# Hybrid encoder, layer 0: the end of the recurrent stage reordered, with part of the output product among the scan steps

## The chip, the cores and the metric
One core of a Trainium2 chip, one launch. The metric is the device time in microseconds (us). PE is TensorE, PEld its weight loads, DVE VectorE, ACT ScalarE, POOL GpSimd, SP the queue that issues the loads.

## What is computed
Two encoder layers on x (512 tokens, 1024 wide) with 256 memory tokens. The change touches layer 0's mixer:
```python
for t in tokens:                       # both directions, 8 heads of 64
    sa = S @ -kk[t]
    S = S*w[t] + outer(sa, kk[t]*a[t]) + outer(v[t], k[t])
    y[t] = S @ r[t]
y = rms_norm(y_fwd + y_bwd, out_gain)  # over each head's 64
a_out = (y + sum(r*k*r_k)*v) * g       # g = sigmoid(gl) @ g2
b_out = u * spatial_gate(v_sgu)
x = x + concat(a_out, b_out) @ ab_w_out
```

## The kernel before, in words
All large products run as three float32r products of high and low parts. A weight slab (4 blocks of 128 rows, 512 columns, 1 MB) is loaded by SP into WRAW[i % 2], ACT copies its high part (`split_hi`, L330), DVE subtracts the low part (`split_lo`, L338), and PE multiplies (`gemm_pe`, L373). `fence` is the number of the first slab of the output product "ab". It has four slabs: rows 512 to 1023 (the SGU half, whose input HHI/HLO[4:8] is ready before the recurrent stage) for both column halves, then rows 0 to 511 for both. Each slab is 48 matmuls in four banks.

The recurrence runs in chunks of 64 tokens, for four pairs of heads, j = 0 to 3 (`pair_pe`, `pair_act`, `pair_dve`, `pair_pool`). A pair is:
- gram (L884, L896; `gram_dve`): products of AR, BET and KAP; DVE masks them out of PSUM into AI, UU, GBR, GKA, GKR, adds the identity to AI and UU (L1233, L1235) and writes TT (L1237);
- five levels `lv` of an inversion by doubling: PE UU x AI (L990), DVE XX (L1282), PE with XX and TT (L1004, L1007), ACT copies UU, TT (L1122, L1126);
- the tail: WU, RT, PT, QT, YL (L1023, L1031, L1061).

After each half level stand one side step s = 0 to 9 (`side_pe`, `side_act`: the bonus sum, LoRA products and turns for this and the next pair) and one scan step of the pair before (`chain_pe`, `chain_dve`; L913 the state, L921 the output). DVE prepares the next pair's operands in levels 2 to 4 (L1153 to L1192), POOL makes BET (`beta_pool`) and multiplies PT and RT by decay ends (`decay`). Every order is written out by hand, each engine's queue runs in order, and semaphores tie them.

After the fourth pair: seven scan steps alone (`chain_end_pe`), a meeting of the four engines, then `fin_*`: squares, a bones product per pair (L1305), Sqrt on ACT, RECIPROCAL on DVE (L1335), gain, bonus, gates (L1306, g), high and low parts. SP waits for the last pair's QT products before it loads slab `fence`; the slabs and X share the space of the stage's tiles.

## Time and profile before

| what | value |
|---|---|
| median of 3 runs | 1855.76 us (1854.86 to 1858.3) |
| the profiled execution | 1856.78 us, span 1855.0 us |
| PE, DVE, ACT, POOL busy | 95%, 53%, 41%, 6% of the span |
| mean granted clock | 0.988 |
| four pairs | 169.3 to 386.4 us |
| last scan steps | 386.4 to 394.2 us |
| up to the end of "ab" | 394.2 to 459.6 us |

A row gives the line of the kernel, the engine, the operation and output<-input. In groups, the columns are busy us, mean ns of one, and idle time of the engine just before them with what ended it. "issue" is time in which the engine waited for nothing that the profile shows. PEclk is the granted TensorE clock as a share of 2.4 GHz.

### The profile page before, as it was taken

Reading aid. Unit: us, or ns where it says so; the run is one execution under the profiler, and the core shown is the slowest. Engines: PE = TensorE matmul, PEld = TensorE weight load, DVE = VectorE, ACT = ScalarE, POOL = GpSimd, SP = SyncE. Lnnn points to the kernel's source line nnn. Section 1 sums busy time; section 2 is a strip of 40 time slices with the busy share of each in tenths; the row PEclk is TensorE's granted clock in tenths of the full one; section 3 lists DMA queues with packets and bytes.
Section 4 is the critical chain, followed back from the end, with each engine's and each line's share of the span. In section 5 each row is a group of like instructions: output and inputs, shape, how many; then the busy total and the mean of one; then the engine's idle time right before and its main releaser. Section 6 shows DMA issues by size and latency. Waiting matters only on the chain.

```text
span 1855.0 us, 32043 instructions
## 1 busy us (share of the span) xinstructions
PE 1754.3 (95%) x14153; PEld 1439.4 (78%) x14153; DVE 992.3 (53%) x1373; ACT 769.3 (41%) x1182; POOL 108.5 (6%) x87
## 2 busy tenths in 40 slices
PE   6997888889999999999999999989999999999999
PEld 5876777767887788888887887557888878888887
DVE  5477656457534556534645244994634356634552
ACT  4243444334554343413433234873655244422431
POOL 1001221000010000000000022000010000000000
PEclk9999999989999999999999999999999999999999
DMA  7210000033331223333222322002322223222221
GB/s 240 80 46 2 4 4 4 4 137 124 136 114 46 69 91 91 108 98 109 95 69 91 108 76 89 1 1 91 117 98 81 91 68 104 101 91 91 91 89 71
DMA packets 96454, 149.41 MB, mean 81 GB/s; under 512 B 3480, under 2 KB 50171, under 8 KB 96315
## 3 DMA queue, kind: packets, MB, share of 16 engines
q1 hardware_dynamic: 94727, 142.29, 23.3%
q0 software_dynamic: 1296, 4.95, 0.8%
q8 instruction: 111, 1.82, 0.4%
q14 instruction: 29, 0.23, 0.0%
q10 hardware_dynamic: 291, 0.12, 0.0%
HBM read 145.25 MB, written 2.10 MB: 79 GB/s over the span
## 4 chain that ended last, share of the span: by engine, by line
PE 82%; DVE 10%; ACT 4%; issue 3%; DMA 1%; POOL 1%; DVEq 0%; POOLq 0%; SPq 0%; ACTq 0%
PE PS L373 68%; DVE SS L1608 1%; PE PS L531 1%; PE PS L1004 1%; PE PS L1397 1%; PE PS L1366 1%; PE PS L990 1%; DVE WLO L338 1%; PE PS L1031 1%; PE PS L1023 1%; PE PS L636 1%; ACT WHI L330 1%; DMA WRAW<-cross_wq 1%; DVE YQ L1335 1%; PE PS L913 1%
## 5 line engine op out<-in xcount | busy, mean ns | idle before, releaser
L338 DVE TENSOR_TENSOR WLO<-WRAW,WHI 128x2048 fp32r<-128x2048 f32 (+1 forms) x132 | 296.9, 2251 | 455.0 <-ACT WHI L330 455.0
L330 ACT ACTIVATE WHI<-WRAW 128x2048 fp32r<-128x2048 f32 (+1 forms) x132 | 248.1, 1880 | 431.2 <-PE PS L373 404.5
L373 PE MATMUL PS<-HIS,WHI 128*128 128x512 f32 x856 | 333.8, 390 | 1.5 <-DVE SM L1770 1.5
L373 PE MATMUL PS<-HIS,WLO 128*128 128x512 f32 x856 | 333.0, 389 | 0.0
L373 PE MATMUL PS<-LOS,WHI 128*128 128x512 f32 x856 | 333.0, 389 | 0.0
L373 PE MATMUL PS<-WHI,HIS 128*128 128x512 f32 x608 | 238.8, 393 | 4.2 <-DVE WLO L338 3.5
L373 PE MATMUL PS<-WLO,HIS 128*128 128x512 f32 x608 | 237.4, 390 | 0.0
L373 PE MATMUL PS<-WHI,LOS 128*128 128x512 f32 x608 | 237.3, 390 | 0.0
L373 PEld LDWEIGHTS PS<-HIS,WHI 128*128 128x128 f32 x856 | 160.7, 188 | 35.1 <-DVE SM L1770 1.7
L373 PEld LDWEIGHTS PS<-HIS,WLO 128*128 128x128 f32 x856 | 160.7, 188 | 33.7
L373 PEld LDWEIGHTS PS<-LOS,WHI 128*128 128x128 f32 x856 | 160.7, 188 | 33.2 <-issue 0.2
L373 PEld LDWEIGHTS PS<-WHI,HIS 128*128 128x128 f32 x608 | 114.6, 188 | 29.6 <-DVE WLO L338 3.9
L373 PE MATMUL PS<-WHI,GHI 128*128 128x512 f32 x352 | 136.9, 389 | 0.0
L373 PE MATMUL PS<-WHI,GLO 128*128 128x512 f32 x352 | 136.9, 389 | 0.0
L373 PE MATMUL PS<-WLO,GHI 128*128 128x512 f32 x352 | 136.9, 389 | 0.0
L373 PEld LDWEIGHTS PS<-WLO,HIS 128*128 128x128 f32 x608 | 114.6, 188 | 24.0
L373 PEld LDWEIGHTS PS<-WHI,LOS 128*128 128x128 f32 x608 | 114.5, 188 | 23.4
L538 DVE TENSOR_TENSOR X<-X,PS 128x512 f32<-128x512 f32 x64 | 43.1, 685 | 66.3 <-PE PS L373 66.2
L373 PEld LDWEIGHTS PS<-WLO,GHI 128*128 128x128 f32 x352 | 66.1, 188 | 13.8
L373 PEld LDWEIGHTS PS<-WHI,GHI 128*128 128x128 f32 x352 | 66.1, 188 | 13.7
L373 PEld LDWEIGHTS PS<-WHI,GLO 128*128 128x128 f32 x352 | 66.1, 188 | 13.6
L1483 ACT ACTIVATE GHI<-SG 128x512 fp32r<-128x512 f32 x44 | 27.8, 633 | 108.6 <-DVE SG L1503 108.6
(283 smaller groups left out, 2474.1 us busy)
## 6 DMA issues: line engine op xcount, KB each, us to landing
WRAW<-ffn_w_up SPq DMA_DIRECT2D x88, 512.0 KB, 4.7
WRAW<-ffn_w_down SPq DMA_DIRECT2D x20, 1024.0 KB, 5.0
WRAW<-cross_wkv SPq DMA_DIRECT2D x16, 1024.0 KB, 5.1
WRAW<-diff_w_in SPq DMA_DIRECT2D x12, 1024.0 KB, 5.1
WRAW<-ab_w_in SPq DMA_DIRECT2D x10, 1024.0 KB, 5.5
WRAW<-cross_wq SPq DMA_DIRECT2D x8, 1024.0 KB, 5.1
WRAW<-cross_wo SPq DMA_DIRECT2D x8, 1024.0 KB, 5.1
X<-x SPq DMA_DIRECT2D x8, 512.0 KB, 7.2
```

Source lines behind the costliest of these rows:

```text
L330: A.e.activation(part(WHI[i % 3], i), part(WRAW[i % 2], i), ACT.Copy).then_inc(S("w_hi"), 1)
L338: V.e.tensor_tensor(part(WLO[i % 3], i), part(WRAW[i % 2], i), part(WHI[i % 3], i).bitcast(F32), ALU.subtract).then_inc(S("w_lo"), 1)
L373: mm = e.matmul(o, l, r, start=(si == 0 and kk == 0 and q == 0), stop=(si == len(steps) - 1 and kk == nk - 1 and q == 2))
L531: mm = e.transpose(PS[:, norm_bank(b0, k), t * P:t * P + P], xn[:, t, k * P:k * P + P], ident)
L538: V.e.tensor_tensor(o, o, PS[:, bank_base(name, gi) + b, :], ALU.add).then_inc(sem(name, "ev"), 1)
L636: mm = e.transpose(PS[:, bank0 + k % 4, t * P:t * P + P], tok[:, t, k * P:k * P + P], ident)
L913: mm = e.matmul(PS[half(hh), 4, d * HD:d * HD + HD], PT[half(hh), d, o[d][0], :], QT[half(hh), d, o[d][1], :], start=True, stop=True)
L990: mm = e.matmul(PS[xs(x if lv == 0 else 1 - x), 2 * d, u * CH:u * CH + CH], AI[xs(x), d, u, :], UU[xs(x), d, u, :], start=True, stop=True)
L1004: mm_u = e.matmul(PS[xs(y if lv == 0 else 1 - y), 2 * d, u * CH:u * CH + CH], TT[xs(y), d, u, :], XX[xs(y), d, u, :], start=True, stop=True)
L1023: mm = e.matmul(PS[xs(x), 2 * d + u // 4, (u % 4) * P:(u % 4) * P + P], UU[xs(x), d, u, :], AXT[xs(x), d, u, :], start=True, stop=True)
L1031: mm = e.matmul(PS[half(hh), b + x, col0 + t * CH:col0 + t * CH + CH], l(d, hh, t, x), r(d, hh, t, x), start=first == "each" or first == " ...
L1483: A.e.activation(GHI[2 * gi + b - 2][:, :], SG[b - 2][:, :], ACT.Copy).then_inc(sem(name, "hi"), 1)
```

## The change
Masks of the gram become `copy_predicated` onto tiles AI and U0 that hold the identity from the start (`unit_dve`). Side steps move one step later, and the last pair's free ones take the gates. DVE prepares between the two scan steps of a level. The norm keeps one value per token and head: the mean by narrow matmuls, the root by a power on POOL, spread by transposes. The first SGU slab, in a fourth place (WHI3, WLO3, over TMP), is multiplied among the last scan steps; POOL splits the second one; the two meetings go.

```diff
+    WHI = [sb(f"WHI{i}", [P, 4, 512], 32768 + 16384 * i, F32R) for i in range(3)] + [sb("WHI3", [P, 4, 512], 8192, F32R)]
+    WLO = [sb(f"WLO{i}", [P, 4, 512], 32768 + 16384 * i + 8192, F32R) for i in range(3)] + [sb("WLO3", [P, 4, 512], 0, F32R)]
...
+    U0 = sb("U0", [P, 2, 8, CH], r3 + 28672)
...
+    YGN, YSQ, RB = ZS[0:4], ZS[4:8], ZS[12:14]
...
+    def place(i):
+        return i % 3 if i < fence else 3 if i == fence else (i - fence - 1) % 3
...
+    def hi_part(A):
+        i = A.split
+        A.e.wait_ge(S(f"raw_in{i % 2}"), raw_level[i])
+        A.e.activation(part(WHI[place(i)], i), part(WRAW[i % 2], i), ACT.Copy).then_inc(S("w_hi"), 1)
+        A.split += 1
+    def lo_part(V):
+        i = V.split
+        V.e.wait_ge(S("w_hi"), i + 1)
+        V.e.tensor_tensor(part(WLO[place(i)], i), part(WRAW[i % 2], i), part(WHI[place(i)], i).bitcast(F32),
+                          ALU.subtract).then_inc(S("w_lo"), 1)
+        V.split += 1
...
+            if 3 <= i < fence or i >= fence + 4:
...
+    def gates_pe(e, g0):
+        for g in (g0, g0 + 1):
+            e.matmul(PS[:, 6 + g % 2, :], WL2[:, 2, g * P:g * P + P], ZS[ZG][:, :], start=True, stop=True)\
+                .then_inc(S("f_gate"), 1)
...
     def side_pe(T, j, s):
...
-        if s == 1:
+        if s == 2:
             e.wait_ge(S("p_gfree"), 2 * (j + 1))
+            e.wait_ge(S("p_bonus"), j + 1)
...
             mm.then_inc(S("p_bonmm"), 1)
-        elif s == 2:
+        elif s == 3:
+            e.wait_ge(S("p_bonfree"), j + 1)
             if j + 1 < NJ:
-                e.wait_ge(S("p_bonfree"), j + 1)
                 lora_pe(e, j + 1, 0, 6)
-        elif s == 3:
+            else:
+                gates_pe(e, 0)
+        elif s == 4:
             if j + 1 < NJ:
                 e.wait_ge(S("p_lorafree"), 2 * j + 3)
                 lora_pe(e, j + 1, 1, 6)
-        elif s == 4:
+            else:
+                e.wait_ge(S("f_gg"), 2)
+                e.wait_ge(S("f_bg"), 2)
+                gates_pe(e, 2)
+        elif s == 5:
             if j + 1 < NJ:
                 e.wait_ge(S("p_lorafree"), 2 * j + 4)
             else:
-                e.wait_ge(S("p_bonfree"), j + 1)
+                e.wait_ge(S("f_gg"), NJ)
+                e.wait_ge(S("f_bg"), NJ)
...
             mm.then_inc(S("p_tok"), 1)
-        elif s in (5, 6):
...
+        elif s in (6, 7):
+            e.wait_ge(S("p_tokfree"), 3 * j + s - 5)
...
-                    mm = e.transpose(PS[:, 6 + d, t * P:t * P + P], (BET, KAP)[s - 5][:, d, t * P:t * P + P], ident)
+                    mm = e.transpose(PS[:, 6 + d, t * P:t * P + P], (BET, KAP)[s - 6][:, d, t * P:t * P + P], ident)
...
-                                      UU[xs(x), d, u, :], start=True, stop=True)
+                                      (UU if lv > 0 else U0)[xs(x), d, u, :], start=True, stop=True)
...
     def chain_end_pe(T):
...
+        e = T.e
+        units = [(b, kk) for b in range(NT) for kk in range(4)]
+        first = (0, 3, 6, 8, 10, 12, 14, 16)
...
+            chain_pe(e, NJ - 1, i)
+            if i == 1:
+                e.wait_ge(S("w_lo"), fence + 1)
+                e.wait_ge(S("sgu_lo"), SGU_G)
+            for b, kk in units[first[i - 1]:first[i]]:
+                mm = bank_pe(e, "ab", 0, 0, b, [kk], hhi, hlo)
+            if i == NCH - 1:
+                mm.then_inc(sem("ab", "wused"), 1)
+            if i == 1:
+                fin_mean_pe(e, range(NJ - 1))
+            elif i == 4:
+                fin_spread_pe(e, 0, 7)
+                fin_spread_pe(e, 1, 6)
+            elif i == 6:
+                e.wait_ge(S("f_z"), 1)
+                fin_spread_pe(e, 2, 7)
+        e.wait_ge(S("c_yfree"), NJ * STEPS)
...
+    def fin_mean_pe(e, pairs):
+        for j in pairs:
+            e.wait_ge(S("f_sq"), j + 1)
+            for t in range(NT):
+                mm = e.matmul(PS[:, 6, 8 * j + 2 * t:8 * j + 2 * t + 2], YSQ[j][:, t * P:t * P + P], rk("bones")[:, ::HD],
+                              start=True, stop=True)
+        mm.then_inc(S("f_mm"), 1)
+    def fin_spread_pe(e, j, bank):
+        e.wait_ge(S("f_rb"), j + 1)
+        for t in range(NT):
+            mm = e.transpose(PS[:, bank, t * P:t * P + P], RB[j % 2][:, t * P:t * P + P], ident)
+        mm.then_inc(S("f_bc"), 1)
...
+        def amid(gi, si, b):
+            if (gi, si, b) == (1, 0, 1):
+                T.e.wait_ge(S("f_z"), 2)
+                fin_mean_pe(T.e, [NJ - 1])
+            elif (gi, si, b) == (1, 0, 2):
+                T.e.wait_ge(S("f_z"), 3)
+                fin_spread_pe(T.e, NJ - 1, 7)
+            elif (gi, si, b) == (1, 0, 3):
+                T.e.wait_ge(S("f_z"), NJ)
+            turn(gi, si, b)
...
     def side_act(A, j, s):
...
-        if s == 1:
+        if s == 1 and j + 1 == NJ:
+            e.wait_ge(S("p_bonus"), NJ)
+            fin_square_act(e, 0)
+            fin_square_act(e, 1)
+        elif s == 2:
             e.wait_ge(S("p_bonmm"), j + 1)
             e.activation(BON[j][:, :], PS[:, 6, :], ACT.Copy).then_inc(S("p_bonfree"), 1)
-        elif s in (2, 3):
+        elif s in (3, 4):
             if j + 1 < NJ:
-                prep_tanh_act(e, j + 1, s - 2, 6)
-        elif s == 4:
+                prep_tanh_act(e, j + 1, s - 3, 6)
+            else:
+                fin_gate_act(e, 2 * s - 6)
+                fin_gate_act(e, 2 * s - 5)
+        elif s == 5:
             e.wait_ge(S("p_tok"), 3 * j + 1)
...
-        elif s in (5, 6):
-            e.wait_ge(S("p_tok"), 3 * j + s - 3)
+        elif s in (6, 7):
...
-                i = e.activation((BPD, KPD)[s - 5][:, d, :, :], PS[:, 6 + d, :].rearrange("p (t k) -> p t k", k=P), ACT.Copy)
+                i = e.activation((BPD, KPD)[s - 6][:, d, :, :], PS[:, 6 + d, :].rearrange("p (t k) -> p t k", k=P), ACT.Copy)
...
-        elif s == 7:
-            if j + 1 < NJ:
+            if s == 7 and j + 1 < NJ:
                 prep_exp_act(e, j + 1)
+            elif s == 7:
+                e.wait_ge(S("p_bet"), NJ)
+                hi_part(A)
+        elif s == 9 and j + 1 == NJ:
+            e.wait_ge(S("c_yfree"), j * STEPS)
+            fin_square_act(e, j - 1)
...
     def prep_scale_dve(V, j):
...
                                    chunks(TMP[0][:, d, :])[:, :, by], ALU.mult, ALU.mult)
-            e.tensor_scalar(chunks(ar[:, d, 0, :])[:, :, first], chunks(KK[:, j, :])[:, :, first], -1.0, None, ALU.mult)
+            own = chunks(KK[:, j, :])[:, :, first]
+            e.scalar_tensor_tensor(chunks(ar[:, d, 0, :])[:, :, first], own, -2.0, own, ALU.mult, ALU.add)
         e.tensor_tensor(ar[:, :, 1, :], r, TMP[0][:, :, :], ALU.mult)
         for d, last in ((0, CH - 1), (1, 0)):
-            e.tensor_copy(ecl(d, j), TMP[0][:, d, last::CH])
+            own = TMP[0][:, d, last::CH]
+            e.scalar_tensor_tensor(ecl(d, j), own, 0.0, own, ALU.mult, ALU.add)
...
+        e.wait_ge(S("p_bk"), j + 1)
+        e.scalar_tensor_tensor(TMP[1][:, :, :], TMP[3][:, :, :], col("rwkv_r_k", j), r, ALU.mult, ALU.mult)\
+            .then_inc(S("p_bonus"), 1)
...
     def pair_pool(G):
...
-            decay(G.e, j - 1)
+            G.e.wait_ge(S("p_rfree"), j)
+            G.e.wait_ge(S("p_pfree"), j)
+            decay_p(G.e, j - 1)
+            decay_r(G.e, j - 1)
+            G.e.wait_ge(S("p_bonfree"), j)
+            bonus_value_pool(G.e, j - 1)
...
+    def unit_dve(V):
+        for m in (AI, U0):
+            for d in range(2):
+                V.mine(V.e.tensor_copy(m[:, d, :, :], mask8("ident2")))
+        V.wait_mine()
...
     def gram_dve(V, j):
...
-            e.tensor_tensor(units(AI[:, d, :, :]), banks2(4, d * 256, 256).rearrange("p b (t k) -> p b t k", k=CH),
-                            mask24(M_LT[d]), ALU.mult).then_inc(S("p_afree"), 1)
+            e.copy_predicated(units(AI[:, d, :, :]), where24(M_LT[d]),
+                              banks2(4, d * 256, 256).rearrange("p b (t k) -> p b t k", k=CH)).then_inc(S("p_afree"), 1)
         for d, b in ((0, 6), (1, 0)):
             e.wait_ge(S("p_g"), 4 * j + d + 1)
-            V.mine(e.tensor_tensor(units(UU[:, d, :, :]), part2(b, 0), mask24(M_U1[d]), ALU.mult))
+            e.copy_predicated(units(U0[:, d, :, :]), where24(M_U1[d]), part2(b, 0)).then_inc(S(f"p_u{d}"), 1)
             e.tensor_tensor(units(GBR[:, d, :, :]), part2(b, 1), mask24(M_INC[d]), ALU.mult).then_inc(S("p_bfree"), 1)
         e.wait_ge(S("p_afree"), 2 * j + 2)
-        for d in range(2):
-            V.mine(e.tensor_tensor(AI[:, d, :, :], AI[:, d, :, :], mask8("ident2"), ALU.add))
-            V.wait_mine()
-            e.tensor_tensor(UU[:, d, :, :], UU[:, d, :, :], mask8("ident2"), ALU.add).then_inc(S(f"p_u{d}"), 1)
         for d in range(2):
             e.tensor_tensor(TT[:, d, :, :], AI[:, d, :, :], mask8(M_T1[d]), ALU.mult).then_inc(S("p_tt"), 1)
...
+    def decay_p(e, j):
+        for d, lo, hi, prev in decay_ends(j):
+            i = e.tensor_tensor(PT[:, d, lo:hi, :], PT[:, d, lo:hi, :], prev, ALU.mult)
+        i.then_inc(S("p_pt"), 1)
+    def decay_r(e, j):
+        for d, lo, hi, prev in decay_ends(j):
             r = RT[:, d, lo * CH:hi * CH].rearrange("p (c t) -> p c t", t=CH)
             i = e.tensor_tensor(r, r, prev, ALU.mult)
-            if d == 1:
-                i.then_inc(S("p_rt"), 1)
+        i.then_inc(S("p_rt"), 1)
...
     def pair_dve(V, j):
...
-            for s in (2 * lv, 2 * lv + 1):
-                if j > 0 and 1 <= s <= STEPS:
-                    chain_dve(e, j - 1, s)
+            if j > 0 and 1 <= 2 * lv <= STEPS:
+                chain_dve(e, j - 1, 2 * lv)
             if j + 1 < NJ and lv >= 2:
                 (prep_scan_dve, prep_key_dve, prep_scale_dve)[lv - 2](V, j + 1)
+            if j + 1 == NJ and lv in (1, 2):
+                fin_bonus_dve(e, 2 * lv - 2)
+                fin_bonus_dve(e, 2 * lv - 1)
+            elif j + 1 == NJ and lv == 4:
+                e.wait_ge(S("p_bonmm"), NJ)
+                lo_part(V)
+            if j > 0 and 2 * lv + 1 <= STEPS:
+                chain_dve(e, j - 1, 2 * lv + 1)
...
     def chain_end_dve(V):
...
+        e.wait_ge(S("p_pfree"), NJ)
+        decay_p(e, NJ - 1)
         e.wait_ge(S("p_yfree"), NJ)
-        decay(e, NJ - 1)
...
+            if i == 1:
+                e.wait_ge(S("f_mm"), 1)
+                fin_var_dve(e, 0, NJ - 1)
+            elif i == 4:
+                fin_out_dve(V, 0, 7)
+            elif i == 5:
+                fin_out_dve(V, 1, 6)
+            elif i == 7:
+                fin_out_dve(V, 2, 7)
...
+    def fin_square_act(e, j):
+        e.activation(YSQ[j][:, :], YL[:, j, :], ACT.Square).then_inc(S("f_sq"), 1)
+    def fin_gate_act(e, g):
+        e.wait_ge(S("f_gate"), g + 1)
+        e.activation(YGN[g][:, :], PS[:, 6 + g % 2, :], ACT.Copy, scale=col("rwkv_out_gain", g)).then_inc(S("f_gg"), 1)
+    def fin_wide_act(e, j):
+        e.wait_ge(S("f_rstd"), 1 if j < NJ - 1 else 2)
+        if j >= 2:
+            e.wait_ge(S("f_bc"), j - 1)
+        e.activation(RB[j % 2][:, :].rearrange("p (u k) -> p u k", k=HD),
+                     SM[:, 160 + 8 * j:168 + 8 * j].unsqueeze(2).to_broadcast([P, 8, HD]), ACT.Copy).then_inc(S("f_rb"), 1)
+    def fin_hi_act(e, j):
+        e.wait_ge(S("f_out"), j + 1)
+        e.activation(HHI[j][:, :], YSQ[j][:, :], ACT.Copy).then_inc(S("f_hi"), 1)
     def fin_act(A):
...
+        e.wait_ge(S("p_rfree"), NJ)
+        hi_part(A)
+        fin_wide_act(e, 0)
+        fin_wide_act(e, 1)
+        e.wait_ge(S("p_q"), NJ)
+        hi_part(A)
+        fin_wide_act(e, 2)
+        for j in range(NJ - 1):
+            fin_hi_act(e, j)
+        e.wait_ge(S("c_yfree"), NJ * STEPS)
+        fin_square_act(e, NJ - 1)
+        fin_wide_act(e, NJ - 1)
+        fin_hi_act(e, NJ - 1)
...
+    def fin_bonus_dve(e, g):
+        e.wait_ge(S("f_gg"), g + 1)
+        e.wait_ge(S("f_bv"), g + 1)
+        e.tensor_tensor(BON[g][:, :], BON[g][:, :], PS[:, 6 + g % 2, :], ALU.mult).then_inc(S("f_bg"), 1)
+    def fin_var_dve(e, j0, j1):
+        e.tensor_scalar(SM[:, 32 + 8 * j0:32 + 8 * j1], PS[:, 6, 8 * j0:8 * j1], 1.0 / HD, EPS, ALU.mult, ALU.add)\
+            .then_inc(S("f_var"), 1)
+    def fin_out_dve(V, j, bank):
+        e = V.e
+        e.wait_ge(S("f_bc"), j + 1)
+        if j < NJ - 1:
+            e.wait_ge(S("f_yg"), j + 1)
+        e.tensor_tensor(YSQ[j][:, :], YGN[j][:, :], PS[:, bank, :], ALU.mult).then_inc(S("f_z"), 1)
+        e.wait_ge(S("f_z"), j + 1)
+        e.tensor_tensor(YSQ[j][:, :], YSQ[j][:, :], BON[j][:, :], ALU.add).then_inc(S("f_out"), 1)
+    def fin_lo_dve(e, j):
+        e.wait_ge(S("f_hi"), j + 1)
+        e.tensor_tensor(HLO[j][:, :], YSQ[j][:, :], HHI[j][:, :].bitcast(F32), ALU.subtract).then_inc(S("f_lo"), 1)
...
     def fin_dve(V):
...
+        V.mine(e.tensor_tensor(YGN[NJ - 1][:, :], YGN[NJ - 1][:, :], YL[:, NJ - 1, :], ALU.mult))
+        for j in range(NJ - 1):
+            fin_lo_dve(e, j)
+        e.wait_ge(S("f_mm"), 2)
+        fin_var_dve(e, NJ - 1, NJ)
+        V.split += 1
+        e.wait_ge(S("w_lo"), fence + 2)
+        lo_part(V)
+        V.wait_mine()
+        fin_out_dve(V, NJ - 1, 7)
+        fin_lo_dve(e, NJ - 1)
...
+        e = G.e
+        e.wait_ge(S("p_bonfree"), NJ)
+        bonus_value_pool(e, NJ - 1)
+        for j in range(NJ - 1):
+            e.wait_ge(S("f_gg"), j + 1)
+            e.wait_ge(S("c_yfree"), (j + 1) * STEPS)
+            e.tensor_tensor(YGN[j][:, :], YGN[j][:, :], YL[:, j, :], ALU.mult).then_inc(S("f_yg"), 1)
+        e.wait_ge(S("p_rfree"), NJ)
+        decay_r(e, NJ - 1)
+        fin_pow_pool(e, 0, NJ - 1)
+        e.wait_ge(S("w_lo"), fence + 1)
+        e.wait_ge(S("p_q"), NJ)
+        G.split = fence + 1
+        lo_part(G)
+        fin_pow_pool(e, NJ - 1, NJ)
...
+    def fin_pow_pool(e, j0, j1):
+        e.wait_ge(S("f_var"), 1 if j0 == 0 else 2)
+        e.tensor_tensor(SM[:, 160 + 8 * j0:160 + 8 * j1], SM[:, 32 + 8 * j0:32 + 8 * j1],
+                        SM[:, 16:17].to_broadcast([P, 8 * (j1 - j0)]), ALU.pow).then_inc(S("f_rstd"), 1)
+    def bonus_value_pool(e, j):
+        e.tensor_tensor(BON[j][:, :], BON[j][:, :], ZS[ZV + j][:, :], ALU.mult).then_inc(S("f_bv"), 1)
...
-                gemm_pe(T, "ab", hhi, hlo, operand=lambda k: (S("f_lo"), NJ) if k <= NJ else (S("sgu_lo"), SGU_G),
-                        amid=mem_turn_pe(T, 0))
+                gemm_pe(T, "ab", hhi, hlo, operand=lambda k: (S("f_lo"), NJ), amid=mix_beside_pe(T),
+                        only=[(1, 0), (0, 1), (1, 1)])
...
-                    e.wait_ge(S("p_q"), NJ)
+                    e.wait_ge(S("p_rfree"), NJ - 1)
+                if i == fence + 1:
+                    e.wait_ge(S("p_tok"), 3 * NJ)
                 if i >= 2:
                     e.wait_ge(S("w_lo"), i - 1)
                 load_slab(e, i)
-                if i == fence + 1:
+                if i == fence + 3:
+                    e.wait_ge(*used_at[fence])
                     load_x(e)
```

## Rows read from the trace of the kernel before
**Rows 1.** Busy time by stage (window; per engine us and instructions; PEclk; DMA share; GB/s).
```profile
169.30:222.20 52.90, 45.23 (x1691) 40.28 (x1687) 32.66 (x47) 23.40 (x39) 9.46 (x7) 0.98 0.02 4
222.20:276.80 54.60, 45.11 (x1724) 40.22 (x1720) 33.32 (x56) 22.61 (x38) 9.49 (x7) 1.00 0.02 4
276.80:335.20 58.40, 48.47 (x1759) 43.25 (x1752) 34.49 (x58) 23.04 (x39) 10.39 (x8) 0.97 0.02 4
335.20:386.40 51.20, 42.59 (x1675) 38.91 (x1667) 24.68 (x47) 18.37 (x32) 0.00 (x0) 1.00 0.03 5
...
320.40:335.20 14.80, 10.70 (x522) 10.35 (x522) 5.67 (x11) 4.27 (x6) 3.61 (x4) 1.00 0.01 4
...
386.40:394.20 7.80, 6.98 (x104) 5.96 (x104) 3.74 (x14) 1.91 (x1) 0.00 (x0) 0.59 0.96 364
394.20:433.50 39.30, 31.99 (x112) 21.98 (x112) 33.42 (x28) 16.43 (x20) 1.34 (x2) 0.91 0.32 115
408.00:430.00 22.00, 21.98 (x96) 17.93 (x96) 19.93 (x16) 4.91 (x6) 0.83 (x2) 1.00 0.14 48
433.50:446.30 12.80, 12.80 (x49) 10.46 (x50) 6.24 (x5) 4.10 (x5) 0.00 (x0) 0.87 0.61 213
446.30:459.60 13.30, 13.03 (x66) 10.69 (x66) 9.57 (x17) 8.39 (x15) 0.72 (x1) 1.00 0.41 149
```
**Rows 2.** Groups of instructions on DVE, recurrent stage and what follows it.
```profile
L1229 DVE TENSOR_TENSOR UU<-PS,RC 128x512 f32<-128x512 f32 x6 | 4.1, 685 | 1.7 <-PE PS L896 1.7
...
L1155 DVE TENSOR_TENSOR_SCAN TMP<-RC,TMP 128x512 f32<-128x512 f32 x2 | 2.4, 1224 | 0.1
...
L1335 DVE RECIPROCAL YQ<-YQ 128x512 f32<-128x512 f32 x4 | 13.4, 3347 | 1.6 <-ACT YQ L1318 1.6
```
**Rows 3.** PE's waits, 169.3 to 386.4 (us in total, times, longest).
```profile
PE PS L1004 <- DVE XX L1282: 8.2, 8, 2.2
PE PS L1061 <- issue: 6.5, 4, 1.6
PE PS L990 <- DVE UU L1235: 4.8, 8, 1.3
PE PS L1031 <- issue: 4.4, 4, 1.3
PE PS L941 <- DVE GKR L1244: 3.4, 4, 0.9
```
**Rows 4.** Timeline of DVE: first gram, third tail, fourth gram (in brackets: idle before).
```profile
169.33 1.29 DVE L1225 TENSOR_TENSOR AI<-PS,RC 128x512 f32<-128x512 f32 x2 [2.29 <-PE PS L884]
...
325.71 1.29 DVE L1250 TENSOR_TENSOR RT<-PS,AR 128x512 f32<-128x512 f32 x2 [2.24 <-PE PS L1031]
...
338.78 0.68 DVE L1233 TENSOR_TENSOR AI<-AI,RC 128x512 f32<-128x512 f32 x1
```
**Rows 5.** Timeline of PE: KAP's turns, a T product, the gates.
```profile
306.62 1.09 PE L966 MATMUL PS<-KC,KAP 128*128 128x128 f32 x8
...
310.25 0.27 PE L1004 MATMUL PS<-XX,TT 64*64 64x64 f32 x1 [1.93 <-DVE XX L1282]
...
399.14 1.91 PE L1306 MATMUL PS<-ZS,WL 128*128 128x512 f32 x2
...
404.54 1.02 PE L1306 MATMUL PS<-ZS,WL 128*128 128x512 f32 x2
```
**Rows 6.** Groups on POOL: powers of two widths.
```profile
L625 POOL TENSOR_TENSOR SM<-SM 128x64 f32<-128x64 f32 x2 | 21.1, 10529 | 107.7 <-DVE SM L557 107.7
...
L453 POOL TENSOR_TENSOR SM<-SM 128x4 f32<-128x4 f32 x3 | 3.0, 1014 | 43.9 <-DVE SM L458 43.9
```
**Rows 7.** Timeline of POOL and DVE, third pair.
```profile
304.34 2.35 POOL L1203 TENSOR_TENSOR BET<-KK,TMP 128x1024 f32<-128x1024 f32 x1 [4.56 <-PE PS L966]
...
305.17 2.08 DVE L1153 TENSOR_SCALAR TMP<-TMP 128x1024 f32<-128x1024 f32 x1
...
314.09 0.81 DVE L1167 TENSOR_SCALAR TMP<-TMP,COLS,SM 128x1024 f32<-128x1024 f32 x1
```

127 lines of the change are left out of this document (35 added, 92 removed).

## The prediction
> **How I read the profile.** I went from the share of the span by engine to the table by stage, then to PE's waits in the stage that is edited, then to single rows for prices. TensorE is busy 95% of the span, so only stages where it waits or works at the low clock can give much. The table by stage [rows 1] shows two of them: the four pairs of the recurrent stage (169.3 to 386.4, four rows, 217.1 us) and what follows up to the end of the "ab" product (386.4 to 459.6, 73.2 us). In that second part the 7.8 us of scan steps run at a granted clock of 0.59, and the 39.3 us after them hold only 22.0 us of product (the row of 408.0 to 430.0: 96 matmuls, 0.229 us each at full clock); the rest is the norm and the gates, with a RECIPROCAL of 3.35 us on each pair's path [rows 2], and two idle stretches of PE. From 433.5 on PE runs without a break. Nothing behind 459.6 is edited, and PE is full there, so I count the change as what it takes from these two stretches, against the profiled execution: 1856.78 us (span 1855.0). That is 1.0 above the median of 1855.76.
>
> **The pairs.** PE's waits that have a named cause are, over the four pairs, 8.2 us on XX, 4.8 on the UU that L1235 writes and 3.4 on GKR before the bonus sum [rows 3]; 16.4 together.
> - Gram: of DVE's operations from AI to TT, four go (L1233 and L1235 for both directions, 0.6 to 0.7 each [rows 4]); the masked products become copy_predicated. PE may start level 0 once the second GBR is written, and DVE writes TT beside PE's first products. So the 4.8 goes, and the 0.7 per pair that PE waits for the first XX (2.7 of the 8.2).
> - Bonus: the sum moves from side step 1 to 2, where GKR is long written, so the 3.4 goes. LoRA, token turns, BET and KAP turns each move one step later. Every one of them still has its matmuls; only the neighbours change. Next late would be the exponentials on ACT, which now stand behind the KPD copies, and POOL's last BET product behind them; it is wanted only by the next gram, with the last level and the tail between, so I cost it at nothing.
> - Preparation on DVE: today both scan steps' additions come before it, so XX of the next level waits behind (1.9 us at 310.25 in the third pair [rows 5]; with the next level's and the second pair's, the other 5.5 of the 8.2). After, it runs between the two additions, beside PE's T products. Its longest piece (2.08 [rows 7] and two scans of 1.22 [rows 2], 4.5 us) fits in there; the bonus product that is moved behind KAP (1024 columns, at most twice 0.69) falls in DVE's 2.2 us of idle before the tail [rows 4]. The 5.5 goes.
> - Added: the four products for the gates (0.43 us each at full clock [rows 5]) leave the end and enter the last pair: +1.7. Four identity copies at the start, at most 0.69 each, stand against 2.3 us in which DVE waits for the first gram [rows 4]: +0.3. BON times V moves to POOL between decay and the next pair's rates, where POOL idles.
> - The unknown price is copy_predicated, sixteen of them, all on the path before level 0. The trace has none. From below: no less than the product it replaces, 0.69 [rows 2], as it streams the same 512 columns out of PSUM. From above: the scan at 1.22 or the RECIPROCAL at 3.35 for the same shape [rows 2]. I take 0.69, for it selects and does not iterate.
> - Given back: PE also stops with the cause "issue", 6.5 us at L1061 and 4.4 at L1031 [rows 3], always in the tail where nothing holds it. Between 320.4 and 335.2 it got through 1044 instructions in 14.8 us, 14.2 ns each [rows 1]; the pairs as wholes take 15.3 to 16.6 ns. Taking 14.2 as what the instruction stream gives, the second pair (3444 instructions, 54.6 us) can't fall below 48.9. There is room for 14 us in all, but in places the stream will be late instead: between nothing and all of it, I take 3.
>
> Pairs: 16.4 - 1.7 - 0.3 - 3 = 11.4 us.
>
> **The end.** T0 = 386.4, when QT is copied (DVE's decay halves, but PE and the QT copy were last, so T0 itself gains nothing from it).
> 1. Seven scan steps cost 7.8 us at clock 0.59, 1.1 each; at full clock I estimate 0.76: 5.3. Among them stand the 48 matmuls of the first SGU slab: 11.0. PE begins at the low clock as now; nine matmuls at 433.5 show what such a start costs (12.8 us for 48 instead of 11.0, clock 0.87 [rows 1]): +2.0.
> 2. Twelve small matmuls for the means and twelve transposes for the spread, at 0.13 (eight in 1.09, the last overlapping what follows [rows 5]): 3.1. The chain ends at T0 + 21.4.
> 3. The second SGU slab with the last pair's mean and spread: 11.0 + 1.0, T0 + 33.4. Third slab 11.0. Fourth 13.3 as now, with the memory's turns: T0 + 57.7.
>
> *What must be ready.* The norm's root is now a power on POOL: 128x64 took 10.53 us, 128x4 1.01 [rows 6], so 0.159 per column and 4.2 us for 24 columns, starting near T0 + 6.9: done T0 + 11.1, two wide copies on ACT (0.6 each) T0 + 12.4; PE reaches the first spread at T0 + 13.4. Then POOL splits the second slab: 2.35 us for 1024 columns [rows 7], so about 4.7 for 2048, T0 + 16, wanted at T0 + 21.4. The last pair: variance 0.2, power 1.65, wide 0.6 beside one bank of 2.7 us; product, add, high part 2.1 beside the next; the low part 0.7 beside the last. X is loaded from T0 + 21.4 and is wanted at T0 + 36; the later slabs' splits keep 5 us or more. SP's waits are earlier than before for the first slab (p_rfree of the third pair instead of p_q of the last) and for the second.
> *The lock.* DVE's TENSOR_SCALAR at 305.17 took 2.08 us while POOL's product ran from 304.34 to 306.69; the same shape took 0.81 at 314.09 [rows 7]. POOL's 4.7 us split falls on DVE's BON addition, and the scan's state addition is queued behind it: it ends at T0 + 16 at the latest, and PE wants that state at T0 + 16.6. With the other narrow places (1.0 us at the first spread, 0.3 at the last) I add 0.6.
> The Trainium skill ("SBUF — State Buffer", the single rule on the shared port) says that a DVE instruction with two SBUF inputs and a GpSimd instruction exclude each other for whole instructions; the 1.27 us lost at 305.17 agree. By that rule an addition that comes just after POOL's start waits all of its 4.7 us, and my sum would be 3 us longer; it also says that the products of a tile with itself, put in for the small TENSOR_SCALARs, don't escape POOL.
>
> End: 58.3 instead of 73.2: 14.9 us.
>
> **Sum.** 11.4 + 14.9 = 26.3 us off 1856.78 is 1830.5; with half of the distance to the median, 1830.
>
> **Rivals.**
> - *The predicate at scan price.* Each copy_predicated costs 1.22: +0.53 x 16 = 8.5, less 1 us of slack: 1837.5. For it: it has a mask, data and an old destination. Against: the mask's product has two inputs too. 0.13.
> - *The instruction stream takes back the pairs.* All 14.7 us of removed waits turn up as "issue": 1830 + 11.4 = about 1842. For it: 10.9 us of such stops exist at two lines; slabs now load in the last pair. Against: 14.2 ns is still under every pair's mean. 0.11.
> - *The scan's end waits.* Lock, power or low clock: if the whole chain ran at half clock, 48 x 0.21 + 2 = 12 us more, 1842; if only additions are locked, 1833. In the gates of today PE climbed from 1.91 for two matmuls to 1.02 [rows 5] after some 5 us of unbroken work, which the new end has from its first step. The Trainium skill ("TensorE: Matmul & The Clock Gate", Part 1) has it that activity releases the clock; by it only the beginning is slow, as I summed. 0.12.
> - *Slower than before.* copy_predicated is one of DVE's iterating forms and costs as the RECIPROCAL does, 3.35: 16 x 2.66 = 42.6 us on the gram's path, 1830 + 42.6 - 2 = about 1871. It turns to slower than before by 0.2% from some 2.7 us per instruction. Against: only one row of DVE's is that slow. 0.03.
> - *It doesn't do what it says.* If the first slab weren't split in time (the split waits for a bonus sum, a load and p_bet), the products would stand behind the chain as now and only the norm's path is shorter: about 1845. 0.03, and 0.02 for no change at all.
> - *More*: no stops at "issue" and a full clock from T0: 1824. 0.06.
>
> Mine has 0.50. What a measurement of this kernel can tell from no change is about 0.2%, 3.7 us. Faster: all but the slow one and the case of no change, 0.95; same 0.02; slower 0.03. Range: up to 1843, past the two rivals at 1842, down to 1822, below the last rival.
>
> **What would show it.** In the changed trace: copy_predicated near 0.69; no PE wait on UU, nor on GKR before the bonus sum, XX waits under 2 us in total; "issue" 18 to 24 us; the pairs 204 to 208 us; chain from QT to the second slab 21 to 23 us at a clock over 0.85; the pow on 24 columns 4.2 and POOL's split 4.7; DVE's addition held by it. I am wrong if the pairs keep 215, if PE waits in the chain for f_rb, or if a slab's split is late behind it.

## The result, and the profile after

The changed kernel took 1842.17 us (median of 4 runs, 1837.14 to 1843.89) against 1855.83 for the kernel before: ratio 0.9918, 95% interval 0.9899 to 0.9938. A second series on another occasion (a2_again, below) gave 1839.92 (6 runs, 1837.44 to 1844.82), ratio 0.9911 (0.9894 to 0.9928). Faster, as forecast, inside the range of 1822 to 1843, but 10 to 12 us above the 1830: the gain is about half to two thirds of the 26 us that were forecast.

The profiled execution took 1837.14 us (span 1835.3), 19.6 less than that of before. It is the shortest of its series, so it sits nearer to the forecast than the median does. The page's span and its line of engines:

```profile
span 1835.3 us, 32123 instructions
...
PE 1746.8 (95%) x14193; PEld 1436.9 (78%) x14193; DVE 972.2 (53%) x1353; ACT 766.4 (42%) x1180; POOL 131.1 (7%) x99
```

The shares hardly move; the stages tell more. The table by stage, in the columns of [rows 1]:

```profile
169.30:217.60 48.30, 43.89 (x1654) 39.29 (x1650) 31.11 (x40) 23.51 (x39) 10.00 (x7) 0.99 0.02 5
217.60:272.70 55.10, 46.03 (x1759) 41.24 (x1751) 34.62 (x53) 22.88 (x39) 11.16 (x9) 1.00 0.02 4
272.70:326.00 53.30, 45.76 (x1761) 41.19 (x1755) 34.51 (x54) 22.75 (x39) 12.33 (x10) 1.00 0.07 24
326.00:380.60 54.60, 46.33 (x1684) 40.71 (x1675) 25.84 (x46) 23.97 (x41) 6.89 (x6) 1.00 0.13 43
380.60:400.60 20.00, 19.83 (x186) 16.15 (x187) 6.97 (x19) 6.71 (x8) 8.71 (x2) 1.00 0.15 54
400.60:414.00 13.40, 11.57 (x57) 9.43 (x56) 7.54 (x10) 4.11 (x5) 4.30 (x3) 1.00 0.63 235
414.00:440.40 26.40, 26.13 (x125) 21.55 (x124) 16.73 (x22) 12.84 (x21) 1.41 (x2) 1.00 0.50 177
```

The pairs end at 380.7 instead of 386.3 (QT copied): 211.3 us for 217.0, a gain of 5.7. From there to the last addition of "ab" it is 59.0 us for 73.2, a gain of 14.2. What follows is unchanged (1395.6 and 1395.5). So the end came as forecast and the pairs did not: the last pair is 3.5 us longer than before, the first three 9.2 shorter.

TensorE's waits in the pairs, 169.4 to 381 (us in total, times, longest), next to [rows 3]:

```profile
PE PS L1094 <- issue: 6.3, 4, 1.6
PE PS L1064 <- issue: 6.1, 5, 1.7
PE PS L916 <- issue: 3.0, 3, 1.3
PE PS L1040 <- issue: 3.0, 2, 1.6
PE PS L1037 <- issue: 2.3, 3, 1.4
...
PE PS L1056 <- ACT UU L1218: 0.7, 1, 0.7
```

All waits with a named cause are gone but 0.7 us (16.7 before). The waits called issue went from 17.7 to 27.1 us. Last, single rows of DVE and POOL, the prices that the forecast rested on ([rows 2], [rows 6], [rows 7]):

```profile
169.38 1.33 DVE L1337 COPY_PREDICATED AI<-RC,PS 128x512 f32<-128x512 int32 x2 [0.59 <-PE PS L904]
170.83 0.74 DVE L1341 COPY_PREDICATED U<-RC,PS 128x512 f32<-128x512 int32 x1
...
386.59 4.17 POOL L1519 TENSOR_TENSOR SM<-SM 128x24 f32<-128x24 f32 x1 [11.36 <-DVE SM L1469]
390.74 4.57 POOL L335 TENSOR_TENSOR WLO<-WRAW,WHI 128x2048 fp32r<-128x2048 f32 x1
394.77 1.08 DVE L1479 TENSOR_TENSOR ZS<-ZS,BON 128x512 f32<-128x512 f32 x1
404.89 2.29 DVE L335 TENSOR_TENSOR WLO<-WRAW,WHI 128x2048 fp32r<-128x2048 f32 x1
405.05 3.63 POOL L1519 TENSOR_TENSOR SM<-SM 128x8 f32<-128x8 f32 x1 [9.75 <-DVE SM L1469]
```

A copy_predicated costs 0.73 to 0.74 us, 0.04 to 0.05 more than the product that it replaces (0.69). The power of 24 columns and POOL's split of the slab come out at the forecast 4.2 and 4.7. The power of 8 columns is 3.63 instead of 1.65.

### The profile page after: what moved, and what is told of

The parts are those of the page before. It is cut to its first block, busy times and chain, and to the rows that moved or that the text cites. A ratio compares the mean times of both kernels' runs of the same rounds, so it can differ in the third digit from the quotient of the medians.

```text
span 1835.3 us, 32123 instructions
## 1 busy us (share of the span) xinstructions
PE 1746.8 (95%) x14193; PEld 1436.9 (78%) x14193; DVE 972.2 (53%) x1353; ACT 766.4 (42%) x1180; POOL 131.1 (7%) x99
## 4 chain that ended last, share of the span: by engine, by line
PE 85%; DVE 6%; ACT 4%; issue 3%; DMA 1%; POOL 1%; POOLq 0%; SPq 0%; ACTq 0%; DVEq 0%
PE PS L369 69%; PE PS L1023 2%; PE PS L1037 2%; DVE SS L1783 2%; PE PS L548 1%; PE PS L1572 1%; DVE WLO L335 1%; PE PS L1064 1%; PE PS L916 1%; PE PS L1056 1%; PE PS L1541 1%; ACT WHI L329 1%; PE PS L653 1%; PE PS L1696 1%; DMA WRAW<-cross_wq 1%
## 5 line engine op out<-in xcount | busy, mean ns | idle before, releaser
L369 PEld LDWEIGHTS PS<-WHI,GHI 128*128 128x128 f32 x352 | 66.1, 188 | 13.7
L369 PEld LDWEIGHTS PS<-WLO,GHI 128*128 128x128 f32 x352 | 66.1, 188 | 13.7
```

Of the source, the lines that this page charges most:

```text
L369: mm = e.matmul(o, l, r, start=(si == 0 and kk == 0 and q == 0), stop=(si == len(steps) - 1 and kk == nk - 1 and q == 2))
```

## The experiments

Two theories stood against each other for the 5.7 us in the pairs. *Waits*: each removed wait is worth its length, and something else costs time. *Instruction stream*: TensorE can't get its instructions faster, and every removed wait comes back as issue. The kernels named e are the changed kernel with an edit, those named b the kernel before with one. A series has its own runs of the kernel before: 1857.94 for e1 to e4, 1857.96 for e5 to e7 and b1, 1856.19 for b2, e8 and a2, 1854.82 for e9.

**b1 and b2: parts of the change alone.** b1 moves only DVE's preparation:

```diff
-            for s in (2 * lv, 2 * lv + 1):
-                if j > 0 and 1 <= s <= STEPS:
-                    chain_dve(e, j - 1, s)
+            if j > 0 and 1 <= 2 * lv <= STEPS:
+                chain_dve(e, j - 1, 2 * lv)
...
+            if j > 0 and 2 * lv + 1 <= STEPS:
+                chain_dve(e, j - 1, 2 * lv + 1)
```

> The kernel before with one edit: in DVE's levels the next pair's preparation stands between the two scan steps' additions, as in the changed kernel. By the prediction this alone takes the XX waits but for 2.7 us: pairs 5.5 us shorter, 1850. In the changed kernel undoing it cost 5.2 us. Rival 'instruction stream': most of it comes back as issue, 1 to 3 us shorter, 1853 to 1855.

b2 adds the gram of the changed kernel (copy_predicated, AI and U0 holding the unit).

> The kernel before with two edits: the new order of DVE's preparation (as in b1) and the gram by copy_predicated with the unit kept in AI and U0. Side steps, gates, slab load and end as before. By the steps of the prediction the UU waits (4.8 us) and the first XX wait of each pair (2.6) go: pairs 210.6 less 7.4 = 203.2, time 1844 to 1845. Rival 'instruction stream': the stops called issue grow from 19.6 by 3 to 5 us in their place: pairs 206 to 208, time 1848. If it is under the changed kernel's 211.3 in the pairs, what is left over there (the moved side steps, four gate products, a slab load in the last pair) costs the difference.

Measured: b1 1851.67 (ratio 0.9966, 0.9952 to 0.998), b2 1845.24 (0.9934, 0.9917 to 0.9952). Tables by stage, the four pairs of b1, then of b2:

```profile
169.34:219.57 50.23, 43.95 (x1654) 39.38 (x1651) 31.40 (x44) 23.36 (x39) 9.09 (x7) 0.98 0.02 4
219.57:273.78 54.21, 46.02 (x1757) 41.05 (x1752) 34.07 (x58) 22.86 (x39) 9.14 (x8) 1.00 0.02 4
273.78:328.85 55.07, 46.46 (x1759) 41.46 (x1753) 34.56 (x57) 22.97 (x39) 10.02 (x8) 1.00 0.02 4
328.85:379.96 51.11, 42.36 (x1675) 38.80 (x1667) 24.70 (x47) 18.27 (x32) 0.00 (x0) 1.00 0.02 5
```

```profile
170.45:219.19 48.74, 44.32 (x1655) 39.66 (x1651) 29.14 (x41) 23.66 (x39) 8.80 (x7) 0.98 0.02 5
219.19:271.64 52.45, 45.87 (x1756) 41.16 (x1751) 32.01 (x53) 22.93 (x39) 9.38 (x8) 1.00 0.02 5
271.64:323.94 52.30, 45.83 (x1759) 41.31 (x1753) 32.23 (x53) 22.89 (x39) 10.06 (x8) 1.00 0.02 4
323.94:373.07 49.13, 42.36 (x1675) 38.92 (x1667) 22.37 (x43) 18.25 (x32) 0.00 (x0) 1.00 0.02 5
```

The new order is worth 6.4 us in the pairs (210.6), the new gram 8.0 more (202.6); the forecast had 5.5, and 4.8 + 2.7 = 7.5. Of the two together, 14.7 us are named waits that go, 3.1 of which come back as issue (17.7 before, 19.6 in b1, 20.8 in b2). Another 3.0 are busy time (181.4 before, 178.4 in b2), 2.5 of it already in b1, whose third pair has a granted clock of 1.00 where the kernel before had 0.97. So the theory "waits" holds for most of these two parts, and its consequence is plain: **with only two of the edits the pairs are 8.7 us shorter than in the whole change.** The rest of the change costs 8.7 us there.

- In the last pair it costs 5.5: TensorE's busy time grows by 4.0 (46.3 for 42.4), issue by 2.6, and 1.1 of named waits go. TensorE's added work there is the four products of the gates, busy for 4.0 us in the changed kernel (the lines below).
- In the first three it costs 3.1: issue grows by 3.7 (19.9 for 16.2), busy time and named waits fall by 0.6.

```profile
342.29 1.98 PE L957 MATMUL PS<-ZS,WL 128*128 128x512 f32 x4
346.51 1.98 PE L957 MATMUL PS<-ZS,WL 128*128 128x512 f32 x4
```

The 202.6 is from one profile, of b2's fastest run, but the medians agree with it: b2 is 11.0 us under its kernel before, the whole change 13.7 and 16.3, though b2's end takes 72.7 us and the new one 59 to 62 in most profiles.

**e3 and e4: the same parts undone.** e3 puts both scan additions ahead of the preparation again; e4 takes products by the mask and additions of the unit in place of copy_predicated.

> DVE's order in pairs 0 to 2 goes back: both scan additions of a level, then the preparation of the next pair. The forecast gave this order 5.5 us, all of PE's waits on XX in levels 3 and 4. Theory forecast: the waits on XX come back with 5 to 6 us and the kernel is 5 to 6 us slower than the changed one. Theory stream: PE's stops called issue fall by 2 to 4 us as the waits come back, and the kernel is only 1 to 3 us slower.

> The gram's masks are products again and the identity is added by four more DVE operations per pair, as before the change; U0 stays a tile of its own. The forecast gave this part 4.8 + 2.7 = 7.5 us. Theory forecast: waits on U0 and the first XX return with 7 to 8 us, and the kernel is 7 to 8 us slower. Theory stream: 2 to 4 us of it is taken from stops called issue, and it is 4 to 6 us slower. A third outcome, no loss at all, would say that the pairs are bound by PE's stream alone.

e3: 1846.32 (0.9938, 0.9923 to 0.9953), pairs 216.5, 5.2 longer. The named waits did not come back (1.3 us for 0.7) and issue is 27.3 for 27.1. What grew is busy time, 186.0 us for 181.9, at a granted clock of 0.98 for 1.00. So its trace doesn't show that undoing the order costs waits; it mostly shows a lower clock, and whether the order brings that about was not found.

e4: 1849.01 (0.9958, 0.9945 to 0.997), pairs 220.0, 8.7 longer. Named waits grow by 7.8 us to 8.5 (5.2 on U, 2.6 on XX), issue falls by 3.3 to 23.8, and busy time grows by 4.7, again at 0.98. The gram's waits are back as the first theory said, and the stream takes 3.3 of them, as the second said (2 to 4).

**e6: what the waits called issue are.** PT's group of products, repeated:

```diff
-        tail(0, 0, 0, w, bp, "each", "each")
+        for _ in range(60 if j == 0 else 1):
+            tail(0, 0, 0, w, bp, "each", "each")
```

> The first pair's group of 16 products of 64 columns for PT is issued 60 times over, into the same bank and with the same result: 944 more products and 944 more weight loads, with nothing to wait for. Theory 'instruction stream': bursts of about 7 ns per instruction (14 ns per product with its load) broken by stops called issue, 1.2 to 2 us each and a few us apart, 14 to 15 ns per instruction on the mean: the first pair grows by 26 to 29 us. Rival 'the stops belong to the waits and events around the tail': without events the burst goes on, 944 x 14.5 ns, 13 to 15 us more and no new stops.

The group has 16 products, as that text says, but the trace has two MATMUL rows and two LDWEIGHTS rows for each: the page counts 16081 matmuls for 14193. So twice as many instructions were added as it reckons with, 1888 matmuls and as many weight loads. One execution took 1893.9 us, 51.7 more than the median after, or 13.7 ns for each of 3776 instructions. TensorE's timeline inside the repetition, then the window 217 to 267 and the instruction queue in it (packets, MB, share):

```profile
233.68 2.10 PE L1064 MATMUL PS<-BPD,WU 64*64 64x64 f32 x128 [1.36 <-issue]
237.13 2.10 PE L1064 MATMUL PS<-BPD,WU 64*64 64x64 f32 x128 [1.36 <-issue]
240.58 2.10 PE L1064 MATMUL PS<-BPD,WU 64*64 64x64 f32 x128 [1.36 <-issue]
```

```profile
217.00:267.00 50.00, 29.58 (x1731) 27.62 (x1724) 0.00 (x0) 0.00 (x0) 0.00 (x0) 0.97 0.02 4
```

```profile
q8 instruction: 13, 0.21, 1.9%
```

With nothing to wait for, TensorE works through 128 matmul rows with their loads in 2.1 us and then stands for 1.36, every 3.45 us in these lines and every 3.45 to 4.00 in the whole repetition. In 50 us the queue named instruction brought 13 packets, 0.21 MB: 16 KB each, one per 3.8 us and per 266 instructions. The whole run has 126 such packets, the changed kernel 112. One stop per 256 instructions and one packet per 256 to 270: I read the stops as the wait for the next 16 KB, and e8 tests that. At 256 instructions in 3.45 us such a stretch runs at 13.5 ns per instruction, over these 50 us at 14.5, while the 2.1 us between stops are 8.2 ns; the pairs of b2 stand at 14.9 in the second and third.

**e8 and e1: what makes the stream late.** e8 adds transfers to the first three pairs:

```diff
                 if i == fence:
+                    for j in range(NJ - 1):
+                        for n in range(2):
+                            e.wait_ge(S("p_tok"), 3 * j + 2 + n)
+                            e.dma_start(out[0], a["x"][0]).then_inc(S("extra"), 16)
+                            e.wait_ge(S("extra"), 16 * (2 * j + n + 1))
                     e.wait_ge(S("p_rfree"), NJ - 1)
```

> The changed kernel with six extra transfers of 2 MB, input to output in device memory, two in each of the first three pairs, in a queue that has nothing else to do there (the output is written again at the end). Nothing computes with them. Theory: TensorE's instructions come in transfers of 16 KB over the same 16 DMA engines; a transfer beside them makes them late. A load of 2 MB in the last pair cost 2.5 us of stops (e1), so the three pairs grow by 2 to 2.5 us for each transfer, 12 to 15 us in all, all of it as issue. Rival 'the slab load did not matter': under 2 us.

1865.14 us (1.0042, 1.0026 to 1.0057), slower than the kernel before. The pairs took 237.9 us for 211.3. TensorE's waits there:

```profile
PE PS L1094 <- issue: 7.9, 4, 2.7
PE PS L1023 <- issue: 7.8, 4, 5.4
PE PS L1064 <- issue: 7.0, 5, 1.7
PE PS L1037 <- issue: 4.8, 4, 1.9
PE PS L1007 <- issue: 4.5, 2, 4.0
```

All issue waits together are 45.4 us for 27.1, and single ones last up to 5.4 where none was over 1.8. That is 18 of the 26.6 us; the other 9 are busy time, at a granted clock of 0.95 for 1.00. A transfer of 2 MB cost 4.4 us in all, 3.0 of it as stops, more than the 2 to 2.5 expected.

e1 takes the transfer out of the last pair:

```diff
                 if i == fence + 1:
-                    e.wait_ge(S("p_tok"), 3 * NJ)
+                    e.wait_ge(S("p_q"), NJ)
```

> The load of the second SGU slab (and with it of the third) waits for the last pair's QT products, as it did before the change, so no slab moves while the last pair is computed. The question: the pairs gained 5.8 us instead of the 11.4 of the forecast, with PE's stops called issue grown from 17.7 to 24.9 us, and the last pair got longer (51.2 to 54.6 us). Theory load: the slabs' transfers (2 x 1 MB between 360 and 371 us in the changed kernel) hold up PE's instruction stream; then the last pair's stops fall from 7.2 to about 5 us and the pair to 52 us, though the end gets longer by 0 to 4 us, since the second slab's split on POOL starts later. Theory stream: the stops come from PE's own rate of instructions; then the last pair stays at 54 to 55 us and its stops at 6.5 to 8.

1841.91 us (0.9917, 0.99 to 0.9933): no gain over the changed kernel. Yet the last pair is 52.2 us for 54.7. In the changed kernel SP's two slab loads land there at 334 to 402 GB/s, and behind them TensorE stood 1.35 us at 365.32 and 0.69 at 370.69; e1 has neither. What the pair gave, the stretch behind it lost, at a lower clock. The first 20 us of the end in e1, in a2_again, and the first 18.6 in e9:

```profile
381.40:401.40 20.00, 19.84 (x118) 16.51 (x119) 2.43 (x9) 4.92 (x5) 8.71 (x2) 0.59 0.29 106
```

```profile
381.40:401.40 20.00, 19.91 (x174) 16.09 (x174) 5.77 (x17) 6.63 (x7) 8.73 (x2) 0.91 0.15 53
```

```profile
381.42:400.00 18.58, 18.47 (x143) 15.00 (x143) 3.23 (x11) 5.50 (x6) 8.72 (x2) 0.74 0.34 114
```

**a2_again: the spread of the changed kernel.**

> The changed kernel unchanged, for a second profile and a closer median. Its first profiled execution (1837.1) was 4 to 7 us under its other runs. Theory: the granted clock at the start of the end differs from execution to execution (1.00 in that profile, 0.88 from QT to the last product of the stage in e1's, 0.94 to 0.97 in others): this profile shows 60 to 66 us from QT to the last ab product, and the median is 1841 to 1843. Rival: the first was the true one, median 1837 to 1839.

From QT to the last ab product it took 60.6 us, and the last pair 53.6. Over all profiles with products among the scan steps this stretch was 59.0 (clock 1.00), 60.6 (0.97), 60.6 (0.97, e5), 60.5 (0.97, e8), 61.3 (0.97, e2), 62.0 (0.95, e3), 62.1 (0.94, e4), 62.2 (0.95, e6), 63.3 (0.92, e9) and 66.4 (0.88, e1). One level of the clock is half of the other; e1's 0.59 over 20 us is by estimate a loss of 8.2 us against full clock, and it ended 7.4 us later than in the first profile. So nearly the same end costs 59 to 66 us, and the granted clock from QT on goes with it; that is the size of the spread between runs. It isn't all of that spread: the run of 1843.23 had the same mean granted clock (0.993) as the one of 1837.14. What decides the clock was not settled. Of these, both kernels that loaded the slab late had the lowest clocks; two profiles don't show a rule.

**e2: the lock.** The last pair's norm goes ahead of the slab's low part in DVE's queue, so that nothing of DVE's lies beside the power:

```diff
-        V.split += 1
-        e.wait_ge(S("w_lo"), fence + 2)
-        lo_part(V)
         V.wait_mine()
         fin_out_dve(V, NJ - 1, 7)
         fin_lo_dve(e, NJ - 1)
+        V.split += 1
+        e.wait_ge(S("w_lo"), fence + 2)
+        lo_part(V)
```

> DVE makes the last pair's output and low part before it splits the third slab; nothing else changes. Theory lock: the power on 8 columns took 3.63 us instead of 1.65 because DVE's 2.29 us split (two inputs in SBUF) started 0.16 us before it and shut POOL out; now it takes 1.5 to 1.8 us, PE's wait of 1.8 us on the last spread falls below 0.3, and the end is 1.5 to 2 us shorter. Rival: the power takes 3.6 us by itself (a fixed cost of its form), PE's wait stays at 1.8, and the time is the changed kernel's.

1842.65 us (0.9928, 0.9909 to 0.9946), no gain. POOL's power, and TensorE's longest wait from QT to the end of ab:

```profile
405.15 1.65 POOL L1519 TENSOR_TENSOR SM<-SM 128x8 f32<-128x8 f32 x1 [9.75 <-DVE SM L1469]
```

```profile
PE PS L548 <- DVE MXN L478: 2.8, 1, 2.8
```

Alone the power takes 1.65 us, beside DVE's low part 3.63: the cause of the long power is shown. TensorE's wait of 1.8 us at the last spread is gone, and one of 2.8 at the memory's turns (0.3 before) has come. That the low part, moved back in DVE's queue, pushes the work before those turns is the likely cause; it was not tested.

**e7: is it the order in the end that pays?**

```diff
-        first = (0, 3, 6, 8, 10, 12, 14, 16)
+        first = (0, 0, 0, 0, 0, 0, 0, 16)
```

> The changed kernel, but the 48 products of the first SGU slab all stand behind the seventh scan step instead of between the steps; nothing is left out. Theory (as in the prediction): the products between the steps cover the root on POOL, its wide copies and the state's additions. Without them PE waits for each state addition (about 0.3 us, six times) and at the first spread for the root (it is ready some 12 us after QT, the steps get there after about 6): 6 to 8 us more between QT and the second slab, 1847 to 1851, with the waits named QT or RB. Rival 'the end is set by the array alone': the steps already run at their own pace, under 2 us more. A further 2 to 5 us may come from a low granted clock in the steps, as the kernel before had it (0.59).

1849.38 us (0.9949, 0.9931 to 0.9967). From QT on 67.7 us, 8.7 more than in the changed kernel, and its clock is 0.87. Its pairs, which the edit doesn't touch, took 214.4 us (busy 184.4 for 181.9), so part of its time is not the edit's. TensorE's waits there, and the two stretches from QT on:

```profile
PE PS L1136 <- ACT ZS L1440: 3.8, 2, 2.0
PE PS L933 <- DVE QT L949: 1.6, 1, 1.6
```

```profile
384.80:391.00 6.20, 6.12 (x66) 5.91 (x68) 1.25 (x5) 1.78 (x1) 1.24 (x1) 0.67 0.01 3
391.00:410.00 19.00, 15.47 (x111) 12.63 (x108) 10.37 (x19) 5.89 (x8) 7.43 (x2) 0.66 0.17 56
```

The waits for the root and the state come to 3.6 us more than in the changed kernel (5.4 for 1.8), at the places named but smaller than expected. The other 5 us go with the clock: 0.67 up to 391.0, though TensorE is busy for 6.12 of these 6.20 us, and 0.66 for the 19 us after, where it is busy for 15.5. The kernel before had 0.59 in its steps [rows 1]. Products among the steps hide waits and mostly went with a higher clock, but e1 shows that they don't secure it.

**e5: is the array the bound in the pairs?** The bonus sum and the gates keep nearly all their instructions but lose columns (its bonus and gates are other numbers):

```diff
-            for d in range(2):
-                mm = e.matmul(PS[:, 6, :], rk("bones"), TMP[1][:, d, :], start=(d == 0), stop=(d == 1))
+            mm = e.matmul(PS[:, 6, 0:CH], rk("bones"), TMP[1][:, 0, 0:CH], start=True, stop=True)
...
-            e.matmul(PS[:, 6 + g % 2, :], WL2[:, 2, g * P:g * P + P], ZS[ZG][:, :], start=True, stop=True)\
+            e.matmul(PS[:, 6 + g % 2, 0:CH], WL2[:, 2, g * P:g * P + P], ZS[ZG][:, 0:CH], start=True, stop=True)\
```

> The changed kernel with the bonus sum cut from two products of 512 columns to one of 64 in every pair, and the four gate products cut from 512 to 64 columns (what they leave uncomputed makes bonus and gates other numbers; the copies and DVE work behind them stay). Theory 'instruction stream': the pairs are held by how fast TensorE gets its instructions, so taking array time away and leaving the instructions (only 4 fewer) gives back little: the pairs 208 to 211.3 us, issue stops grow, time 1839 to 1842. Rival 'array time': each column costs; 8 products x 0.43 us and 4 x 0.43 for the gates (less an eighth) go, about 4.5 to 7.6 us with the preamble: pairs 204 to 207, time about 1835.

1834.66 us (0.987, 0.9849 to 0.9891): 7.5 under the median after (5.3 under a2_again's), as the rival had it. But the pairs in its profile are 208.4, 2.9 shorter, with 28.6 us of issue, as the stream theory had it, and the profile as a whole, 1835.7, is only 1.5 under that of the changed kernel. It is inconclusive. In the last pair busy time fell by 2.4 us (43.95 for 46.33), yet the pair stayed at 54.4: with the slabs moving beside it, fewer columns came back as stops.

**e9: the side steps, with e1's late slab.** In the first three pairs the side steps move one step earlier:

```diff
     def side_pe(T, j, s):
+        if j + 1 < NJ and s < 8:
+            s = (s + 1) % 8
...
     def side_act(A, j, s):
+        if j + 1 < NJ and s < 8:
+            s = (s + 1) % 8
...
-                    e.wait_ge(S("p_tok"), 3 * NJ)
+                    e.wait_ge(S("p_q"), NJ)
```

> The changed kernel with two edits that show in different stretches. In the first three pairs TensorE's and ScalarE's side steps (bonus sum, LoRA, turns) stand one step earlier, where the kernel before has them; in the last pair the second SGU slab is asked for after the pair, as in e1. Theory: b2 with the old side steps had the first three pairs in 153.4 us, the changed kernel 156.6 and 157.2; the side steps are the difference, though GKR waits of 2 us come back: 153 to 155 us. Rival: not they but POOL's added work (decay, BON times V), which holds DVE up: it stays at 156.6 or more. The last pair: 52 us instead of 53.6 to 54.7, as in e1. Whole time 1836 to 1839 if both hold and the end keeps its clock, against 1840 to 1842 for the changed kernel; 1840 to 1842 if the rival holds.

1839.36 us (0.9912, 0.9892 to 0.9933), the same as the changed kernel. The first three pairs took 159.0 us for 156.6, with a new wait of 3.9 on UU in a level of the inversion, and here the text above is wrong: the edit doesn't restore the old places. TensorE's steps stand as before the change, but ScalarE's two exponentials, in step 7 in both kernels, are now in step 6, ahead of a level's copies of UU instead of behind them. ScalarE and TensorE's wait in e9:

```profile
199.47 1.06 ACT L1170 ACTIVATE TMP<-TMP 128x1024 f32<-128x1024 f32 x1
200.56 1.06 ACT L1172 ACTIVATE TMP<-TMP 128x1024 f32<-128x1024 f32 x1
201.52 0.58 ACT L1222 ACTIVATE UU<-PS 128x512 f32<-128x512 f32 x1
```

```profile
PE PS L1025 <- ACT UU L1222: 3.9, 2, 3.0
```

So the run doesn't clear the side steps. On the contrary, the issue waits of the first three pairs fell from 19.9 us to 16.6, where b2 has 16.2, and the added wait and 2.1 us of busy time, at a clock of 0.98 for 1.00, hide it. By an estimate from these rows, 159.0 less 3.9 and 2.1 is 153.0, about b2's 153.5. The last pair was 51.8, as in e1: the late slab shortens the last pair by 1.4 to 2.8 us, twice.

## Why the prediction was right and where it was wrong

- **Forecast 1830, range and sign.** Sign and range held, the range with some luck: it reached up to 1843 for two rivals that did not come about as told, and the term of the pairs was twice what came. 12 us lie between 1830 and the median. Of these, 5.7 are the pairs (5.7 gained for 11.4), 0.7 the end (14.2 for 14.9), and the other 3 to 5 are the distance of the profiled execution (1837.1) from the medians (1839.9 and 1842.2), for which the clock at the end is the likely cause, not the shown one.
- **Gram.** Right: UU and first XX waits gone. b2 has 8.0 us for this part, 7.5 by the forecast's rows. The unknown price, taken as 0.69, is 0.73; the rivals at 1.22 and 3.35 fell.
- **Preparation.** Right in the kernel before: 5.9 us of named waits go in b1 and 1.9 come back as issue; with the clock it is 6.4 for 5.5 forecast. e3 lost 5.2 undoing it, but not by waits.
- **Bonus.** The wait on GKR went (3.4), but no gain of it is seen. b2, which keeps the old side steps, has 2.0 of that wait and still the shorter pairs.
- **The step that failed: "only the neighbours change", the gates at 1.7, and the transfers costed at nothing.** I summed the moved side steps and last-pair additions as -3.4 + 1.7 + 0.3. They cost 8.7 (8.1 in the second profile), in three parts.
  - *The gates were priced at half.* I took the two rows of 0.43 us at L1306 for two products. The kernel before makes four such products and its trace has eight rows, so one product is two rows, 0.86 us from its start at 404.54 to that of the next product at 405.40, and four cost 3.4 us (estimate) and not 1.7. In the changed kernel's last pair they are busy for 4.0 (L957, under b2 above). With the late slab (e1) the last pair is 3.1 us over b2's, and its account closes: 4.1 more of busy time, 1.0 less of the wait on GKR, issue the same. e5 says only that beside the slabs these columns can't be had back singly.
  - *The slab load in the last pair*, 1.4 to 2.8 us of late instructions (52.2 and 51.8 in e1 and e9 against 54.7 and 53.6 in the two profiles of the changed kernel, mechanism by e6 and e8). The prediction noted SP's earlier waits and asked only whether the slab arrives in time, not whom it hinders.
  - *The first three pairs*, 3.1 us, are stops called issue. The runs point at the moved side steps: there every kernel with them moved and the new gram has 19.2 to 21.2 us of issue (e6 and e8 apart, which add work and transfers), and the two with TensorE's at the old places, b2 and e9, have 16.2 and 16.6. It is not shown alone, since e9 moved the exponentials too. The rival, POOL's work holding DVE up, exists in the rows (the TENSOR_SCALAR L1263 takes 2.23 us in the second and third pair for 0.81 in b2, the scan L1251 2.02 for 1.23), but in e3 both are back at 0.81 and 1.23, as in e9, and issue is still 20.7. Why the same instructions in another order are brought later stays open.
- **"Given back", 3 us.** The issue waits are 27.1 (24.9 in the second profile), above the 18 to 24 forecast, and the cause was only in part the one named. Removing waits alone raised them by 3.1 (b2), which is the 3 of the forecast; the other 4 to 6 came with the rest of the change. The "room for 14 us" was summed wrong: 13675 instructions at 14.2 ns are 194 us, 23 under the 217.1. The 3 was a choice inside that room, not worked out from it.
- **The end.** From QT to the second slab's first product 20.4 us (21.4 forecast). The 2.0 for a low clock did not occur in this execution, and was between 0 and 8 in others; the small products cost more than I summed, for the twelve of the means are 24 rows and took 2.7 us, where they and the twelve transposes were to take 3.1. Second slab 14.3 (12.0), of which 1.8 is the wait behind the long power. Third and fourth together 24.3 to the last addition (24.3, and 0.6 for narrow places).
- **The lock.** The state addition behind the held DVE operation cost nothing in TensorE's rows. The held operation was 1.08 us at 394.77 for 0.69, a loss of 0.4. The power took 3.63 us beside DVE's split, which started 0.16 us ahead of it, and 1.65 without. The rule in the Trainium skill ("SBUF — State Buffer", the single rule on the shared port) is that a DVE instruction with two SBUF inputs and a GpSimd instruction that reads SBUF exclude each other, and whichever starts first keeps the port for its whole instruction. This trace agrees; here DVE came first and POOL waited, the side that I had not counted. By the same rule a product of a tile with itself, which has two SBUF inputs, doesn't escape. The rows agree: of the four L1280 of the second and third pair, 8 elements wide, three took 0.16 to 0.17 us and one, beside POOL's BET product, 2.33. But the single-input form that it replaced didn't escape either: in b2's first pair its two took 2.5 us together. And the TENSOR_SCALAR at 305.17 that the prediction counts for the two-input rule has one input.
- **Rivals.** "The stream takes back the pairs" forecast 1842 and the median is there, but by another road: b2 shows that removed waits were kept. The chain at half clock, 12 us more, was seen in part (e1, +7.4).

## What to carry to other kernels

Cost a transfer by whom it hinders, too: a stretch of small matmuls lives on its instruction packets, and 2 MB beside it cost 1.4 to 4.4 us. Before pricing an operation from a row, count the rows against the calls in the kernel: here one product is two rows. When a bundle of edits gives less than its parts, run the parts on the old kernel; here two of them alone gave 14.4 us in a stretch where all of them gave 5.7. After an experiment, look in its trace whether the edit did only what was meant: e9's didn't. And hold a profile against the spread of its own runs before taking a sum from it: nearly the same end took 59 to 66 us, and the granted clock went with it.

## What the runs showed of the hardware

- TensorE's instructions arrive in packets of 16 KB, one per 256 to 270 instructions. In e6 a packet took 3.45 to 4.00 us, of which 1.36 to 1.91 were a stop, the instructions being short. Other transfers stretch single stops up to 5.4 us (e8).
- A float32 product of this kernel is two MATMUL rows with two weight loads (e6: 944 products more, 1888 rows more; the gates: four products, eight rows). Transposes and the slabs' float32r products are one row each.
- A power on POOL took 4.17 us for 24 columns of 128 partitions and 1.65 for 8, and 3.63 instead of 1.65 beside a DVE subtraction of two SBUF operands.
- The granted clock in the 20 us after the pairs was 0.59 in e1 and 1.00 in the changed kernel, which differ only in when SP asks for a slab. TensorE was busy for 19.84 and 19.83 of the 20 us and got through 118 and 186 matmuls.
